# The first attention of a two-block transformer program: heads' units taken two at a time on every engine

## The reference

```python
proj = jnp.einsum('bsd,de->bse', hn, w_in[l])     # queries, keys, values, gates g_a, g_b
o_a = indexed_sparse_attention(...)   # per head: softmax(q.k masked by the top 64 keys) @ v
o_b = latent_attention(...)           # per head: softmax((qn.kn + qr.kr) * scale, causal) @ v
y_a = jnp.einsum('bsc,cd->bsd', o_a, w_branch_a[l])
y_b = jnp.einsum('bsc,cd->bsd', o_b, w_branch_b[l])
merged = jax.nn.sigmoid(g_a) * y_a + jax.nn.sigmoid(g_b) * y_b
```

## Time and profile before

| | |
|---|---|
| median of three runs | 998.6 us |
| span of the profiled execution | 996.9 us |
| first attention's units in it | from 80.7 to 154.6 us |
| PE busy over the span | 985.1 us (99%) |
| DVE busy | 679.8 us (68%) |
| ACT busy | 542.7 us (54%) |
| granted PE clock | full in all 40 slices |

### The profile page before, as it was taken

One profiled execution on the slowest core, in us unless ns is written; L12 is line 12 of the kernel. 1 busy time (PEld: TensorE's weight loads), 2 busy tenths in 40 slices (PEclk: granted clock), 3 DMA queues, 4 the chain that ended last, 5 costly groups with the idle time before them and its releaser, 6 DMA issues.

```text
span 996.9 us, 15688 instructions
## 1 busy us (share of the span) xinstructions
PE 985.1 (99%) x6368; PEld 845.5 (85%) x6368; DVE 679.8 (68%) x835; ACT 542.7 (54%) x708; POOL 42.9 (4%) x68
## 2 busy tenths in 40 slices
PE   9999999999999999999999999999999999999997
PEld 8887777898888888887889888888899898888886
DVE  5689887688777777777767565656656576555564
ACT  6676664476555565634445444444555555444452
POOL 1210000000000005000000000000000000000000
PEclk9999999999999999999999999999999999999999
DMA  8354335466656555844337565656554446656541
GB/s 304 105 193 157 116 115 184 154 212 212 209 171 207 172 166 166 260 148 153 123 131 259 187 209 191 204 182 204 184 166 137 151 143 215 207 172 208 172 167 42
DMA packets 121427, 175.89 MB, mean 176 GB/s; under 512 B 3183, under 2 KB 89786, under 8 KB 121370
## 3 DMA queue, kind: packets, MB, share of 16 engines
q1 hardware_dynamic: 119004, 168.82, 51.2%
q0 software_dynamic: 1600, 5.09, 1.6%
q10 hardware_dynamic: 766, 1.16, 0.4%
HBM read 173.82 MB, written 1.25 MB: 176 GB/s over the span
## 4 chain that ended last, share of the span: by engine, by line
PE 76%; issue 19%; DVE 2%; DMA 1%; ACT 1%; POOL 1%; SPq 0%; POOLq 0%; DVEq 0%; ACTq 0%
PE ps L1853 22%; PE ps L1903 16%; PE ps L1874 10%; PE ps L1902 7%; PE ps L1890 5%; PE ps L1917 3%; PE ps L1925 2%; DMA raw<-in_w_in 1%; PE ps L2145 1%; PE ps L2340 1%; PE ps L1905 1%; PE ps L1968 1%; PE ps L2173 1%; PE ps L2401 1%; PE ps L2001 1%
## 5 line engine op out<-in xcount | busy, mean ns | idle before, releaser
L1091 DVE TENSOR_TENSOR w_lo<-raw,w_hi 128x2048 fp32r<-128x2048 f32 (+3 forms) x153 | 345.3, 2261 | 125.7 <-ACT w_hi L550 125.4
L1903 PE MATMUL ps<-x_both,w_hi 128*128 128x512 f32 x992 | 342.7, 396 | 0.0
L550 ACT ACTIVATE w_hi<-raw 128x2048 fp32r<-128x2048 f32 (+3 forms) x161 | 302.3, 1879 | 58.9 <-PE ps L1853 40.2
L1902 PE MATMUL ps<-x_both,w_lo 128*128 128x256 f32 x868 | 242.1, 279 | 0.0
L1903 PEld LDWEIGHTS ps<-x_both,w_hi 128*128 128x128 f32 x992 | 179.2, 188 | 34.5
L1902 PEld LDWEIGHTS ps<-x_both,w_lo 128*128 128x128 f32 x868 | 163.6, 189 | 5.6
L805 ACT ACTIVATE work<-ps 128x512 f32<-128x512 f32 x66 | 39.3, 595 | 150.3 <-PE ps L1903 134.5
L1853 PE MATMUL ps<-w_hi,x_both 128*128 128x512 f32 (+1 forms) x320 | 101.6, 388 | 0.2 <-DVE w_lo L1091 0.2
L1853 PE MATMUL ps<-w_hi,hid_hi 128*128 128x512 f32 x240 | 93.8, 391 | 0.0
L1853 PE MATMUL ps<-w_lo,hid_hi 128*128 128x512 f32 x240 | 93.4, 389 | 0.0
L1853 PE MATMUL ps<-w_hi,hid_lo 128*128 128x512 f32 x240 | 93.4, 389 | 0.0
(11 more groups left out here) (297 smaller groups left out, 1283.3 us busy)
## 6 DMA issues: line engine op xcount, KB each, us to landing
raw<-in_ffn_w SPq DMA_DIRECT2D x66, 1024.0 KB, 5.1
raw<-in_w_up SPq DMA_DIRECT2D x22, 1024.0 KB, 5.1
raw<-in_hgrn_w_in SPq DMA_DIRECT2D x16, 1024.0 KB, 5.3
raw<-in_w_in SPq DMA_DIRECT2D x12, 1024.0 KB, 5.4
raw<-in_moba_w_in SPq DMA_DIRECT2D x12, 1024.0 KB, 5.2
raw<-in_w_down SPq DMA_DIRECT2D x11, 1024.0 KB, 5.0
raw<-in_w_out SPq DMA_DIRECT2D x4, 1024.0 KB, 5.1
raw<-in_hgrn_w_out SPq DMA_DIRECT2D x4, 1024.0 KB, 6.3
```

The source lines that it names most:

```text
L550: act.activation(w_hi[:, n % RING, 0:kc * cols], raw[:, n % RING, 0:kc * cols], ACT.Copy).then_inc(s["hi_ready"], 1)
L1091: dve.tensor_tensor(w_lo[:, n % RING, sl], raw[:, n % RING, sl], f32(w_hi[:, n % RING, sl]), ALU.subtract).then_inc(s["lo_ready"], 1)
L1902: pe.matmul(out[:, 0, :], w_lo[:, n % RING, at], x_hi[:, k, :], start=False, stop=False)
L1903: ins = pe.matmul(out, w_hi[:, n % RING, at], x_both[:, k, :, :], start=(k == 0), stop=(k == DC - 1))
```

## The change

Within the first attention, all three engines take units two at a time. PE turns units u and u+1, makes the scores of u+2 and u+3, the values of u-2 and u-1, then does both fillers, which are one whole granule. Scores of units 8 to 15 now lie side by side in the two banks. DVE does the maxima of two units, then their scalings, and then one block of other work (`hidden1`): whole granules' low parts in the place of halves, and the rounds of `largest` at other places. ACT takes its steps in the order that fits. The second unit's scores move ahead, into the middle of the last product before the units. At unit 14 the order on DVE is now: both outputs' low parts, the low part for heads 0 to 3, the low part of granule `ba`, and then `gate_branch_b(0)`. The second attention's code stays as it was. The lists below carry the line numbers of their own kernel; in the changed kernel line 1885 is the dense product (1853 before), 2173 the turns (2145), 2206 the scores (2156), 2223 the values (2173), 1111 the low parts (1091), 1373 and 1375 the maxima (1355 and 1357), 1383 and 1389 the scaling (1368 and 1374), 1422 and 1437 low parts of outputs (1393 and 1408), 1432 the gating (1403) and 1486 the low part for heads 0 to 3 (1442).

```diff
@@ -590,17 +590,37 @@
                 if first == 0:
-                    exps(first)
+                    exps(0)
+                    exps(1)
                     copy_gate(0, G["gate0"] + 1, 6)
+                    for u in range(0, count, 2):
+                        extra(u)
+                        if u >= 2:
+                            output(u - 2)
+                        if u + 2 < count:
+                            exps(u + 2)
+                        if u >= 2:
+                            output(u - 1)
+                        turned_probs(u)
+                        if u + 2 < count:
+                            exps(u + 3)
+                        turned_probs(u + 1)
+                        extra(u + 1)
+                    output(count - 2)
+                    output(count - 1)
+                    return
...
-                if u == 12:
+                if u == 13:
                     act.wait_ge(s["o_copied"], 12)
@@ -1332,14 +1352,12 @@
-                dve.wait_ge(s["scores_done"], u + 1)
+                dve.wait_ge(s["scores_done"], u + 2 if 8 <= u < 16 and u % 2 == 0 else u + 1)
...
+                if first == 0:
+                    maxima(0)
+                    largest()
+                    probs(0)
+                    maxima(1)
+                    probs(1)
+                    for u in range(0, count, 2):
+                        if u + 2 < count:
+                            maxima(u + 2)
+                            maxima(u + 3)
+                            probs(u + 2)
+                        if u >= 2:
+                            after(u - 2)
+                        if u + 2 < count:
+                            probs(u + 3)
+                        if u >= 2:
+                            after(u - 1)
+                        hidden(u)
+                    return
...
             def after1(u):
-                if 2 <= u <= 9:
-                    latent_lo(u - 2)
-                if u in ROUNDS:
+
+                if u < 8:
+                    latent_lo(u)
+                if u in (12, 13):
+                    output_lo1(u)
+
+            def hidden1(u):
+
+                if u == 0:
                     largest()
-                if u == 3:
-                    lo_half(g0 + 2, 1)
-                if u == 6:
+                    lo(g0 + 1)
+                    largest()
+                elif u == 2:
+                    lo(g0 + 2)
+                    largest()
+                    largest()
+                elif u == 4:
+                    largest()
                     choose_keys()
-                if u == 14:
-                    gate_branch_b(0)
-                    output_lo1(12)
-                if u == 15:
+                    lo(g0 + 3)
+                elif u < 14:
+                    if u == 8:
+                        bounds(9)
+                    lo(g0 + u // 2 + 1)
+                    if u == 12:
+                        bounds(12)
+                else:
                     dve.wait_ge(s["ohi_ready"], 1)
                     dve.tensor_tensor(x_lo[:, 0:2, :], o_T[:, 0:2, :], f32(x_hi[:, 0:2, :]), ALU.subtract).then_inc(s["olo_ready"], 1)
-                    output_lo1(13)
-
-            def hidden1(u):
...
+                    lo(ba)
+                    gate_branch_b(0)
@@ -2113,7 +2145,7 @@
-                        pe.wait_ge(s["neg_ready"], u)
+                        pe.wait_ge(s["neg_ready"], u - u % 2)
...
+                if first == 0:
+                    for u in range(0, count, 2):
+                        turn_probs(u)
+                        turn_probs(u + 1)
+                        if u + 2 < count:
+                            score(u + 2)
+                            score(u + 3)
+                        if u >= 2:
+                            value(u - 2)
+                            value(u - 1)
+                        extra(u)
+                        extra(u + 1)
+                    value(count - 2)
+                    value(count - 1)
+                    return
...
-            token_product(G["gate0"] + 1, 4, 6, False, True)
+            token_product(G["gate0"] + 1, 4, 6, False, True, part=0)
+            pe.wait_ge(s["group_copied"], 9)
+            scores1(1).then_inc(s["scores_done"], 1)
+            token_product(G["gate0"] + 1, 4, 6, False, True, part=1)
             pe.wait_ge(s["group_copied"], 11)
             units(0, 16, scores1, values1, lambda u: (prob, TT), filler)
```

More of the change, by code:

```diff
@@ L1359, in units, with probs @@
             def units(first, count, hidden, after):
[L1362 to L1365, removed]
+                def probs(u):
                     c = 2 * (u % 2)
@@ L1375, in units @@
                     ins.then_inc(s["prob_ready"], 1)
+                if first == 0:
[17 more added lines that the diff above has]
+                    return
+                for u in range(first, first + count):
+                    probs(u)
                     after(u)
@@ L1379, in units @@
                     hidden(u)
[L1381 to L1387, removed]
             def latent_lo(u):
@@ L1447, in hidden1 @@
                     largest()
-                elif u == 1:
                     lo(g0 + 1)
+                    largest()
                 elif u == 2:
[L1451 to L1456, removed]
+                    lo(g0 + 2)
[3 more added lines that the diff above has]
+                    largest()
+                    choose_keys()
+                    lo(g0 + 3)
[6 more added lines that the diff above has]
+                else:
+                    dve.wait_ge(s["ohi_ready"], 1)
+                    dve.tensor_tensor(x_lo[:, 0:2, :], o_T[:, 0:2, :], f32(x_hi[:, 0:2, :]), ALU.subtract).then_inc(s["olo_ready"], 1)
+                    lo(ba)
+                    gate_branch_b(0)
             units(0, 16, hidden1, after1)
@@ L2132, in value, with turn_probs @@
                     values(u).then_inc(s["pv_done"], 1)
[L2134 to L2138, removed]
+                def turn_probs(u):
                     pe.wait_ge(s["prob_ready"], u + 1)
@@ L2146, in units @@
                     ins.then_inc(s["probT_done"], 1)
+                if first == 0:
[13 more added lines that the diff above has]
+                    return
+                for u in range(first, first + count):
+                    if u + 1 < first + count:
+                        score(u + 1)
+                    if u > first:
+                        value(u - 1)
+                    turn_probs(u)
                     extra(u)
@@ L2155, in scores1 @@
                         rows = slice(HD * hh, HD * hh + HD)
-                        ins = pe.matmul(ps[:, 2 + hh, 0:S], qa_T[rows, j, P * t:P * t + P], ka_T[rows, j // 2, :], start=True, stop=True)
+                        ins = pe.matmul(ps[:, 2 + hh, S * (u % 2):S * (u % 2) + S], qa_T[rows, j, P * t:P * t + P], ka_T[rows, j // 2, :], start=True, stop=True)
                     return ins
```

16 lines of the change are left out of this document (7 added, 9 removed).

## The result

| | before | changed |
|---|---|---|
| median of the runs | 998.5 us (998.1 to 998.8) | 1008.1 us (1006.0 to 1008.7) |
| ratio | | 1.0092, 95% interval 1.0080 to 1.0104 |
| span of the profiled execution | 996.9 us | 1005.8 us |
| mean granted clock | 0.998 | 0.993 |

The change makes the kernel 0.9% slower. The forecast was 1004.8 in a range of 1001.5 to 1009.0; the result lies in that range, 3.3 us above the forecast. It lies outside the forecast's own range of 1003.0 to 1006.5, and 0.4 us above the higher of the two prices of rival 1 (1006.9 and 1007.7).

What follows compares the result with a forecast made beforehand. PE bounds the kernel (99% busy), with DVE following without slack until the top-k search ends. Waits 9.4, less 3.6, less 0.1, plus 0.4: 998.6 + 6.2 = 1004.8 us; own range 1003.0 to 1006.5, with rivals 1001.5 to 1009.0.

Steps and rivals of the forecast that it cites:

- forecast's own range: Whole kernel: 1003.0 to 1006.5 us for the forecast alone, all three waits and full clock, without the rivals.
- rival 1: PE's clock also falls to half in the wait at filler 14: 1006.9, or 1007.7 us; chance 0.27.
- rival 2: The array pays its switches at each unit, so 3.6 us is not gained: 1008.4 us; chance 0.13.
- Switches, -3.6: On PE, a pair passes once through the array switches that two units passed twice: 3.6 us gained.
- First wait, 1.6: At the first turns, PE waits 1.6 us for DVE's scaling of unit 1's probabilities.
- The wait of 0.1 before unit 7's turns: PE waits 0.1 us just before unit 7's turns, counted beside the second wait.
- Second wait, 2.9: Before filler 6, PE waits 2.9 us (0 to 4.5) for DVE's low part of g0+3, behind choose_keys.
- Third wait, 4.7: Before filler 14, PE waits 4.7 us (3.5 to 5.5) for gate_branch_b(0), queued behind low parts including lo(ba).
- After the units, +0.4: In branch A's product, DVE's steps for the merged row end late for PE: +0.4 us (0 to 0.8).
- The clock, 0 in the forecast: The forecast assumed full clock throughout, with no loss from PE's waits; chance of all three waits and full clock 0.48.
- Slower had 0.91: Chance given to the changed kernel being slower; faster had 0.05, within 0.2% 0.04.

Runs made afterwards that it cites:

- x7_busy6: x1_gate_first with 12 small useless products put on PE just before filler 6: 999.0 us, ratio 1.0004.
- x9_alternate: The mixed one, but inside pairs from unit 8 on turns, scores and values of one unit, then of the other: 998.0 us, ratio 1.0001.
- x5_max1_first: x1_gate_first with the maxima of unit 1 ahead of unit 0's scaling on DVE: 1000.1 us, ratio 1.0015.
- x4_lo3_first: x1_gate_first with the low part of granule g0+3 ahead of the round and the choice of the keys on DVE: 999.0 us, ratio 1.0010.
- x1_gate_first: The changed kernel with gate_branch_b(0) right behind the low part of unit 12's block on DVE: 1001.8 us, ratio 1.0031.
- x2_swap: The changed kernel with gate_branch_b(0) and lo(ba) swapped, nothing else: 1006.3 us, ratio 1.0079.
- the mixed one: Units 0 to 7 one by one as before, pairs from unit 8, gating early, low parts one granule earlier from unit 8: 997.6 us, ratio 0.9988.
- x6_again: The mixed one measured a second time, against the kernel before: 998.5 us, ratio 1.0000.
- x3_busy: The changed kernel with 20 unused matmuls of 128 columns on PE ahead of filler 14's wait: 1004.2 us, ratio 1.0059.

## Why the prediction was right, and where it was not

**The range.** The forecast of 1004.8 had the waits and the switches, and the runs bear out both. The stated range reached up to 1009.0 only because the rivals' prices were taken in; the forecast's own range, 1003.0 to 1006.5, missed the result. By its number alone rival 2 (1008.4, no gain from the switches) was nearest; the traces rule it out.

**Switches, -3.6: right, a little too much.** The changed kernel's distance gives 3.3, and x7_busy6's gives 75.0 - 73.9 = 1.1 = 1.4 + 2.9 - 3.2. A pair saves 9.1 - 8.6 = 0.5 (predicted 0.54). Rival 2 is out, shown by x9_alternate.

**First wait, 1.6: measured 1.4**, with the cause shown by x5_max1_first. The wait of 0.1 before unit 7's turns isn't in the list.

**Second wait, 2.9: measured 2.9.** PE stood from 112.4 (predicted 112.6), DVE's low part ended at 115.2 (115.5). DVE has a gap of 0.55 us for ACT in each of the two masked pairs, for which I had put 0.7. x4_lo3_first shows that the order was only half of it.

**Third wait, 4.7: measured 4.8**, and the queue in front of the gating is as predicted: high part, output, low parts, `lo(ba)`, gating. x1_gate_first and x2_swap show that it is the order. The prediction's own terms give 146.8 for the end of filler 13, not 147.0, and so 4.9.

**After the units, +0.4: measured 0.4, though the span doesn't show it.** The steps add up to 7.5 and not 7.4, so the working gives 0.5 to 0.6; and by the earlier trace rows DVE's two steps before ended about 1.1 us ahead of PE's turns, where the prediction has "late enough". Both kernels take 842.3 from branch A's product on, but the pause of PE in the HGRN part was 1.1 before and 0.5 here. Without it the kernel before has 841.2, the mixed one 841.1, and the eight traces with all units in pairs 841.4 to 842.0.

**The clock, 0 in the forecast: wrong.** The failing step is in rival 1 of the prediction, "it is longer than 3.3. Against: one case doesn't show that each such gap is enough". I took the 3.3 us after the last matmul as the least that a fall needs, so that the wait of 2.9 was no candidate at all, and that of 4.7 came out with 0.27 against 0.48. In the traces the clock fell 2.0 to 2.3 us after PE's last matmul (both falls of the changed kernel and the first of x2_swap), or only 1.1 us after PE was back at work, behind waits of 2.6, 2.9 and 1.8 us (x2_swap, x5_max1_first, x6_again). A wait of 2.9 had no fall in two traces (x1's and x3's). The price in the changed kernel was 1.4 and 1.95, where rival 1 had 2.1 for one fall (4.2 us at half pace); in all traces of the stretch it was 1.4 to 2.9. The rows from which that 2.1 was taken are weaker than they looked: in the trace of before, the granted clock of the first 10 us reads 1.00, so that the clock made those products slow isn't shown.

So rival 1's mechanism was right, and it came twice: 1004.8 + 3.35 = 1008.1, the measured median. That the sum fits so closely is in part chance, since the four runs spread from 1006.0 to 1008.7. x3_busy and x7_busy6 fill the waits with useless products: 1004.2 in place of 1008.1, and 999.0 in place of 1001.8. The Trainium skill ("TensorE: Matmul & The Clock Gate", section "Why this matters for your kernels") says that idle gaps between bursts of matmuls put the clock back to half. The traces agree behind the waits of 4.8 and 2.6 us, and behind that of 2.9 in three traces of five.

**Chances.** Slower had 0.91, and was right. The cases were each priced for themselves; that the forecast's waits and the clock go together was left to one term.

## What to carry to other kernels

Two steps that share a switch of the array's mode save about 0.5 us for each set, which is small beside one wait; before such a pairing look at what the partner engine has in its row, for it must then deliver twice as much at once, and anything urgent behind a long step (here a gating behind a low part) goes in front. A wait of PE can cost more than its own length: here waits of 2.6 to 4.8 us had 1.4 to 2.9 us of clock behind them in most traces, one of 1.8 us at the program's start had 1.7, and waits of 1.4 us and less had none. Cut such a wait in two, fill it with useless products, or count that price as a chance and not as a constant. A kernel's stretch can be compared to 0.1 us in a trace, once the clock's falls are taken out, even where the whole time is uncertain by 1 us; take both.

## What was not expected of the hardware

- The clock fell while PE had stood still for as little as 2.0 us (x2_swap: last matmul to 112.8, fall at 114.8), and did not fall in a wait of 2.9 us in two traces. Three falls came 1.1 us after PE had gone back to work: in x2_swap (154.6 to 155.8, behind a wait of 2.6), x5_max1_first (114.0 to 115.1, behind 2.9) and x6_again (10.1 to 11.2, behind 1.8). The clock came back 3 to 7 us after each fall, with PE at work at half pace for 2.8 (115.3 to 118) to 6.0 us (x2_swap, 115.6 to 121.6).
- Useless products made a kernel faster: 12 of them, 2.8 us of PE's time, took 2.8 us off the median (x1_gate_first, 8 runs; x7_busy6, 10 runs).
- Two places outside the change vary between executions and make up much of the spread of the runs: a wait for a high part near the start (0.4 us in the trace of before, 0.4 to 1.8 in the others, and the 1.8 with a fall of the clock behind it), and a pause in the HGRN part that ends in nothing that the profile shows. The second in the trace of x1_gate_first:

```profile
PE ps L2393 <- issue: 1.7, 1, 1.7
```

It is 1.1 in the trace of before and 0 in those of x2_swap, x3_busy, x5_max1_first and x7_busy6, and its cause is open.
